# Modulation in plain fp32, attention maxima on the whole array, values weighed in groups of up to three

## The reference, cut to what matters

```python
mod = jax.nn.silu(c) @ w_mod[l] + b_mod[l]          # 1024 -> 3072, for c and for c_ctx
shift, scale, gate = jnp.split(mod, 3, axis=-1)
h = rms_norm(x, g_pre) * (1.0 + scale) + shift
z = h @ w_in                                        # q, k, v of both attentions, GLA, gates
s = jnp.einsum('bkgqd,bksd->bkgqs', q, k) * scale   # per head; sample queries see the cache too
p = jax.nn.softmax(s, axis=-1)
o = jnp.einsum('bkgqs,bksd->bkgqd', p, v)
o_c = rms_norm(o_c, c_out_gain)                     # the linear attention's output
x_new = x + gate * rms_norm(mixed @ w_out, g_post)
```

## Time and profile before

| what | us |
|---|---|
| time, median of 3 runs | 2437.39 (2436.99 to 2437.45) |
| the profiled execution | 2432.47, its span 2430.8 |
| modulation, layer 1 and 2 | 9.9 to 65.9, 1225.5 to 1275.9 |
| projection, layer 1 | 72 to 441 |
| attention, layer 1 | 536 to 1073 |
| PE busy in the span | 2159.8 (89%) |
| DVE, ACT, POOL busy | 1395.5, 961.3, 902.0 |

### The profile page before, as it was taken

How to read it: one execution, slowest core, us unless ns; L and a number is a source line. 1 busy time by engine, 2 the same in 40 slices (tenths; PEclk the granted TensorE clock), 3 DMA queues, 4 the chain that set the end, 5 groups by cost and what they waited for, 6 DMA issues and landing times. The chain is left out here.

```text
span 2430.8 us, 29142 instructions
## 1 busy us (share of the span) xinstructions
PE 2159.8 (89%) x10645; PEld 1453.8 (60%) x10645; DVE 1395.5 (57%) x2271; ACT 961.3 (40%) x1910; POOL 902.0 (37%) x490
## 2 busy tenths in 40 slices
PE   4799999888999999959958999998889999999598
PEld 3578888654444444427736789886544444444286
DVE  5668200585666666686556672006856666666864
ACT  5432221424555555541254322214255555555321
POOL 0211111324666666650002111113256666666600
PEclk8999999888999999979978999998899999999799
DMA  7232221110001000023373322211100010000333
GB/s 262 100 118 87 65 69 58 37 42 7 18 19 31 18 16 15 13 92 105 107 256 110 112 87 61 72 59 33 42 7 18 19 31 19 19 19 7 104 104 104
DMA packets 196825, 155.79 MB, mean 64 GB/s; under 512 B 125053, under 2 KB 150081, under 8 KB 196673
## 3 DMA queue, kind: packets, MB, share of 16 engines
q1 hardware_dynamic: 196672, 153.82, 21.2%
HBM read 115.37 MB, written 38.42 MB: 63 GB/s over the span
## 5 line engine op out<-in xcount | busy, mean ns | idle before, releaser
L1176 POOL TENSOR_TENSOR prob_sums<-prob_sums,probs 128x1024 f32<-128x1024 f32 x224 | 537.4, 2399 | 113.0 <-ACT probs L1365 93.2
L1365 ACT ACTIVATE probs<-scores 128x512 f32<-128x512 f32 x672 | 363.5, 605 | 388.1 <-PE scores L1246 205.8
L1426 DVE TENSOR_REDUCE neg_max_parts<-work 128x1 f32<-128x512 f32 (+1 forms) x640 | 398.3, 683 | 203.3 <-PE work L1225 202.4
L526 POOL TENSOR_TENSOR w_lo<-w_stage,w_hi 128x512 fp32r<-128x512 f32 (+1 forms) x112 | 134.5, 1234 | 828.5 <-ACT w_hi L461 828.5
L428 PE MATMUL z_acc<-w_hi,h_hi 128*128 128x512 f32 (+1 forms) x640 | 237.5, 371 | 12.0 <-DVE h_lo L545 8.1
L428 PE MATMUL z_acc<-w_hi,h_lo 128*128 128x512 f32 (+1 forms) x640 | 234.6, 367 | 0.0
L428 PE MATMUL z_acc<-w_lo,h_hi 128*128 128x512 f32 (+1 forms) x640 | 234.4, 366 | 0.0
L850 DVE MEMSET k_stackB<- 128x24 f32 (+1 forms) x4 | 0.9, 218 | 346.6 <-PEq L312 346.6
L1173 POOL TENSOR_TENSOR prob_sums<-probs 128x1024 f32<-128x1024 f32 x32 | 76.3, 2384 | 320.3 <-ACT probs L1365 320.3
L1463 DVE RECIPROCAL recip_sums<-work 128x512 f32<-128x512 f32 x32 | 107.5, 3358 | 144.4 <-PE work L1282 144.4
L428 PE MATMUL z_acc<-h_hi,w_lo 128*128 128x512 f32 (+1 forms) x528 | 187.0, 354 | 0.0
(11 more groups left out here) (244 smaller groups left out, 3894.8 us busy)
## 6 DMA issues: line engine op xcount, KB each, us to landing
mod_w<-in_w_mod SPq DMA_DIRECT2D x24, 1024.0 KB, 7.2
w_stage<-in_w_in SPq DMA_DIRECT2D x96, 256.0 KB, 3.0
z_scratch<-z_out SPq DMA_DIRECT2D x60, 256.0 KB, 2.0
cv<-u_scratch SPq DMA_DIRECT2D x20, 512.0 KB, 6.4
u_scratch<-z_out SPq DMA_DIRECT2D x32, 256.0 KB, 2.0
out_y_sample<-y_tiles SPq DMA_DIRECT2D x16, 512.0 KB, 5.2
q_rawA<-z_scratch SPq DMA_DIRECT2D x16, 320.0 KB, 4.1
vB<-z_scratch SPq DMA_DIRECT2D x16, 320.0 KB, 3.3
```

What stands on the lines that cost most here:

```text
L526: pool.tensor_tensor(w_lo[:, n % RING, 0:cols], stage[:, n % STAGES, 0:cols], w_hi[:, n % RING, 0:cols].bitcast(F32), ALU.subtract).then_i ...
L1176: ins = pool.tensor_tensor(a, a, pr[:, n % NPB, :], ALU.add)
L1365: act.activation(pr[:, n % NPB, c * NB:(c + 1) * NB], sc[m % SCORE_BANKS][:, :], ACT.Exp, scale=SCALE[u]).then_inc(s["a_exp"], 1)
L1426: dve.tensor_reduce(dst, src, AX_X, ALU.max, negate=True).then_inc(s["a_wkdve"], 1)
```

## The change

In the modulation `w_mod` stays whole in SBUF and is multiplied as plain fp32: 48 matmuls of 32 output columns, four of them at four column positions of the array. No rounding, no subtraction. SP issues all big loads at once, the shift and scale columns first, the gate columns last; ACT issues the 18 small ones. In the attention, `scan` goes: each piece 6 to 26 is one matmul over the whole array (128 rows for A, 96 for B). DVE copies pieces 3 to 5 instead of ACT. The maximum is one row instead of two. The steps are weighed in groups of 2, 3, 3, 2 and 1, the pieces are placed by `SLOTS`, `probs` has eight tiles, and `prompt_output` follows the maxima. To make room, three small tiles share the space of `recip_sums`, and `gla_norm` takes one token tile at a time. The prologue makes a small matrix `sel` for the turns, and the halves of `q_stackA2` and `kTA2` change places. Cut to its core:

```diff
@@ modulation_block @@
+            def load_w(k, c0, c1):
+                sp.dma_start(w[:, k, c0:c1], io["w_mod"][bass.ds(l, 1), k * P:(k + 1) * P, c0:c1].rearrange("a p n -> (a p) n")
+                             ).then_inc(s[f"m_w{k}" if c0 == 0 else f"m_g{k}"], 16)
+
+            load_w(0, 0, HEAD)
+            f.load_x(sp, 0)
+            for k in range(1, KD):
+                load_w(k, 0, HEAD)
+            f.load_x(sp, 1)
+            for k in range(KD):
+                load_w(k, HEAD, 3 * D_MODEL)
+            f.load_w(sp, 0, STAGES)
...
+            def products(pair, first, end):
+                for k in (2 * pair, 2 * pair + 1):
+                    pe.wait_ge(s[f"m_w{k}" if first == 0 else f"m_g{k}"], 16)
+                for a in range(first, end):
+                    for c in range(2):
+                        for r in range(2):
+                            x = 32 * (2 * c + r)
+                            n0 = (2 * a + c) * NB
+                            mm = pe.matmul(acc[a][x:x + 32, :], cond[:, 2 * pair + r, :], w[:, 2 * pair + r, n0:n0 + NB],
+                                           start=(pair == 0), stop=(pair == KD // 2 - 1), tile_position=(0, x))
+                    if pair == KD // 2 - 1:
+                        mm.then_inc(s["m_used"], 1)
...
+            pe.wait_ge(s["m_cond"], 2)
+            products(0, 0, 2)
+            pe.wait_ge(s["m_small"], 16 * 18)
+            pe.transpose(bias_tr, rows[:, :], per["ident"][0:NT + 2 * KD, 0:NT + 2 * KD]).then_inc(s["m_tr"], 1)
+            products(1, 0, 2)
+            f.turn(pe, 0)
+            products(2, 0, 2)
+            products(3, 0, 2)
+            turn(0)
+            turn(1)
+            for pair in range(KD // 2):
+                products(pair, 2, 3)
+            turn(2)
...
+            for dst, src in loads:
+                act.dma_start(dst, src).then_inc(s["m_small"], 16)
+            f.square(act, 0)
+            act.wait_ge(s["m_dot"], 2)
+            act.activation(dots[:, :], dots[:, :], ACT.Exp).then_inc(s["m_exp"], 1)
+            for a in range(PARTS):
+                act.wait_ge(s["m_used"], a + 1)
+                act.copy(parts[:, a, :], acc[a][:, :]).then_inc(s["m_evac"], 1)
+                if a == 1:
+                    f.square(act, 1)
...
+            def add_bias(out, a):
+                for g in range(2):
+                    do(dve.tensor_tensor(out[:, g, :].rearrange("p (c m) -> p c m", c=2), cols[a][:, :, :, g].rearrange("p m c -> p c m"),
+                                         bcols[:, a * KD:(a + 1) * KD].rearrange("p (c m) -> p c m", c=2), ALU.add))
...
@@ attention @@
-GROUPS = ((0, 1), (2, 3), (4, 5), (6, 7), (8, 9))
+GROUPS = ((0, 1), (2, 3, 4), (5, 6, 7), (8, 9))
 LAST = 10
 UNITS = 2 * A_HEADS
 PREP = 30
 PREP_Q, PREP_MAX, PREP_LAST = 3, 6, 27
-NPB = 6
+NPB = 8
 DIRECT = 1
 SCORE_BANKS, WORK_BANKS = 3, 4
 CHUNKS = 2 * KT_S + 1
-PROMPT_USE = 18
+PROMPT_USE = 27
+SLOTS = (((0, 2), (2, 2), (4, 2), (6, 2)), ((8, 2), (10, 2), (12, 2), (14, 3)), ((17, 3), (20, 3), (23, 4)))
...
-        nm = sb("neg_max", [P, T])
         rs = sb("recip_sums", [P, NB])
-        rsp = sb("recip_prompt", [P, P])
-        csq = sb("c_squares", [P, 2, C_HEADS * C_DV])
-        stats = sb("c_stats", [P, 3, T, C_HEADS])
+        rsp, csq = rs[:, 0:P], rs[:, 0:C_HEADS * C_DV]
+        stats = rs[:, 3 * P:3 * P + 3 * T * C_HEADS].rearrange("p (a t h) -> p a t h", a=3, t=T)
...
-        m_cols = {A: qst2[:, :, 0:2], B: qst[B][:, :, 3 * B_QK:KR[B]]}
+        m_cols = {A: qst2[:, :, HEAD_DIM], B: qst[B][:, :, 3 * B_QK]}
...
+                if i == PREP_MAX:
+                    wait_read(pe, prep_use(p, PREP_MAX - 1))
+                    if fresh(u, h):
+                        wait_read(pe, prep_use(p, PREP_Q - 1))
...
+                    m, rows = i - PREP_MAX, P if u == A else 3 * B_QK
+                    if m < 2 * TS:
+                        parts = [(m // 2, (m % 2) * NB, NB)]
+                    else:
+                        q0 = 2 * (m - 2 * TS)
+                        keys0 = 2 * NB if q0 < TS else KT_S * P
+                        parts = [(q0, keys0, SEQ), (q0 + 1, keys0, SEQ)]
+                    for x, (t, k0, n) in enumerate(parts):
+                        mm = pe.matmul(bank[:, x * SEQ:x * SEQ + n], qT[u][0:rows, tile_rows(t)], kT[u][0:rows, k0:k0 + n],
+                                       start=True, stop=True)
                 mm.then_inc(s["a_work"], 1)
-
-            def max_parts(m):
-
-                if m < 2 * TS:
-                    return [(m // 2, (m % 2) * NB, NB)]
-                q0 = 2 * (m - 2 * TS)
-                keys0 = 2 * NB if q0 < TS else KT_S * P
-                return [(q0, keys0, SEQ), (q0 + 1, keys0, SEQ)]
-
...
-                banks = [work_bank(pe, prep_use(p, i)) for i in pair]
-                parts = [max_parts(i - PREP_MAX) for i in pair]
-                for x in range(len(parts[0])):
-                    for r, bank in enumerate(banks):
-                        t, k0, n = parts[r][x]
-                        rows = slice(r * w, (r + 1) * w)
-                        keys = kT2 if u == A and r else kT[u]
-                        mm = pe.matmul(bank[:, x * SEQ:x * SEQ + n], qT[u][rows, tile_rows(t)], keys[rows, k0:k0 + n],
-                                       start=True, stop=True)
-                        if x == len(parts[0]) - 1:
-                            mm.then_inc(s["a_work"], 1)
...
                 for g in range(len(GROUPS) - 1):
-                    pieces(nxt, 6 * g, 2)
-                    ahead(p, GROUPS[g + 1][0])
-                    pieces(nxt, 6 * g + 2, 2)
-                    ahead(p, GROUPS[g + 1][1])
-                    pieces(nxt, 6 * g + 4, 2)
+                    for piece, step in zip(SLOTS[g], GROUPS[g + 1]):
+                        pieces(nxt, *piece)
+                        ahead(p, step)
+                    pieces(nxt, *SLOTS[g][-1])
                     for i in GROUPS[g]:
                         weigh(p, i)
-                pieces(nxt, 24, 2)
                 ahead(p, LAST)
-                pieces(nxt, 26, 1)
                 for i in GROUPS[-1]:
                     weigh(p, i)
                 pieces(nxt, PREP_LAST, PREP - PREP_LAST)
...
-                        if i in (1, 2, 3):
-                            for x in range(2 * i - 2, 2 * i):
+                        if i in (1, 2):
+                            for x in range(2 * i - 2, min(2 * i, PREP_Q)):
...
+                for i in range(PREP_Q, PREP_MAX):
+                    cols = slice((i - PREP_Q) * NB, min((i - PREP_Q + 1) * NB, TOK))
+                    dve.wait_ge(s["a_work"], worked(p, i))
+                    dve.tensor_copy(qT[u][:, cols], wk[prep_use(p, i) % WORK_BANKS][:, 0:cols.stop - cols.start]
+                                    ).then_inc(s["a_wkdve"], 1)
                 for i in range(PREP_MAX, PREP_LAST):
-                    if p and i == PROMPT_USE:
-                        prompt_output(p - 1)
...
-                dve.tensor_reduce(nm[:, 0:TS], nmx[:, 0:TS, :], AX_X, ALU.min).then_inc(s["a_own"], 1)
-                dve.wait_ge(s["a_own"], 2 * p + 1)
-                mc = m_cols[u]
-                dve.tensor_copy(mc[:, :, 0], nm[:, :]).then_inc(s["a_own"], 1)
-                dve.wait_ge(s["a_own"], 2 * p + 2)
-                dve.tensor_tensor(mc[:, :, 1], nm[:, :], mc[:, :, 0].bitcast(F32), ALU.subtract).then_inc(s["a_nm"], 1)
+                dve.tensor_reduce(m_cols[u][:, 0:TS], nmx[:, 0:TS, :], AX_X, ALU.min).then_inc(s["a_nm"], 1)
+                if p:
+                    prompt_output(p - 1)
...
+                wait_read(dve, prompt_use(p))
...
+                dve.wait_ge(s["a_out"], UNITS)
                 oc = mid["oc"]
-                for t in range(0, T, 2):
-                    do(dve.tensor_tensor(csq[:, :, :], oc[:, t:t + 2, :], oc[:, t:t + 2, :], ALU.mult))
-                    ins = dve.tensor_reduce(stats[:, 0, t:t + 2, :], csq[:, :, :].rearrange("p t (h e) -> p t h e", h=C_HEADS), AX_X,
-                                            ALU.add)
-                    if t + 2 < T:
+                for t in range(T):
+                    do(dve.tensor_tensor(csq, oc[:, t, :], oc[:, t, :], ALU.mult))
+                    ins = dve.tensor_reduce(stats[:, 0, t, :], csq.rearrange("p (h e) -> p h e", h=C_HEADS), AX_X, ALU.add)
+                    if t + 1 < T:
```

More of the change, by code:

```diff
@@ L264, in _ @@
-            f.square(act, 1)
+            C = C_HEADS * C_DK
+            gw = per["gate_w"]
+            loads = [(rows[0:NT, :], layer(io["b_mod"]).rearrange("a (m p) -> (a m) p", p=P)),
+                     (rows[NT:NT + KD, :], layer(io["g_pre"]).rearrange("a (m p) -> (a m) p", p=P)),
+                     (rows[NT + KD:, :], layer(io["g_post"]).rearrange("a (m p) -> (a m) p", p=P))]
+            loads += [(lams[:, i, :], layer(io[name]).broadcast_to([P, B_QK]))
```

(46 more changed lines are left out.)

188 lines of the change are left out of this document (57 added, 131 removed).

## The result

The change made the kernel slower: a median of 2447.97 us (2447.09 to 2449.76, 5 runs) against 2437.12 (2434.42 to 2437.45, 5 runs) in the same session, a ratio of 1.0048 (95% interval 1.0033 to 1.0062). The profiled execution's span is 2446.7 us at a mean granted clock of 0.942, against 2430.8 at 0.950.

The account below looks back on a forecast made before the run. PE was taken to bound the attention, with DVE's loop close behind, and queued loads the modulation; -22.5 - 25.6 + 15.4 + 7 = -25.7 gave 2406.8 profiled, 2412 us as median, forecast range 2395 to 2428, overall range 2364 to 2436.

Parts of the forecast that it names:

- B units: Attention units followed by an A unit: 30.3 us against 29.22, +1.1 each, +15.4 for 14; bounds -1.5 to +3.
- the modulation: Both layers' modulation bound by the load stream: -14.1 and -8.4, together -22.5; bounds -30 to -9.
- A units: Attention units followed by a B unit: 31.55 us against 33.17, -1.6 each, -25.6 for 16; bounds -2.9 to 0.
- unit 15: Last unit of each layer: ten half-size squares and sums in `gla_norm`, +3.5 per layer, +7 together; bounds +2 to +10.
- the wait behind `split_hi`: B unit: `split_hi` holds ACT for 1.6 us and so PE for 1.3.
- the clock falls: Rival: PE's new waits in B units bring back 1.2 GHz, 14 x 2.8 = 39, 2451 us; chance 0.10.
- lies between: B unit: PE's wait, 1.9 us beside 1.3, lies between harmless sub-microsecond waits and the 7.82 followed by a slow score.
- pieces and scores to 21.75: A unit layout: after three steps weighed to 17.35, PE's pieces and scores end 21.75 us into the unit.
- Worth little in PE time: Whole-array maxima in place of side-by-side pairs: 21 x 0.23 = 4.8 us for about 6.0 of PE time.
- PE waits for them after its first products, with 20 us to spare: Modulation: PE's wait for the small loads issued by ACT was to leave 20 us to spare.
- a rival with that size: Modulation doesn't get its stream: column tiles run serially or small loads hold all up; -9, 2425 us; chance 0.12.
- POOL and the copies: DVE's three query copies take 1.65 us; rival: POOL slows each by 0.9, +81, 2493 us, chance 0.03.

Follow-up runs that it names:

- filled_wait: Kernel after with the last score ahead of the first maxima made seven times over, into the same place; 2444.9 us (ratio to before 1.0032).
- late_pieces: Kernel after with the first two pieces of maxima moved behind the weighing of tiles 0 and 1; 2405.22 us (ratio to before 0.9876).
- whole_only: Kernel before with the maxima as whole-array matmuls in the same places and the query turn copied whole by ACT; 2412.7 us (0.9901).
- mod_late: Kernel before with the new modulation alone, its small-load wait and bias turn moved behind the fourth pair of products; 2416.8 us (0.9924).
- norm_pairs: Kernel after with the squares of the c branch made two tiles at a time, as in before; 2447.26 us (ratio to before 1.0051).
- q_on_act: Kernel after with the first query turns copied by ACT again instead of DVE; 2438.86 us (ratio to before 1.0014).
- whole_best: whole_only with the modulation of mod_late and ACT's square root moved from step 5 to step 8 of the last unit; 2388.82 us (0.9813).

## Why the prediction was wrong, step by step

The prediction put the profiled execution 25.7 below before; it came out 15.9 above. The 41.6 between are made of these terms: ordinary B units 12 x (3.26 - 1.1) = 26, the modulation 11, A units with the starts of the attention 10, less 3 for the two fresh units and less 2 for unit 15 and the rest.

**B units: the mechanism was right, two sizes were off.** PE's wait for the copies, which was to end 6.6 us into the unit, ended at 6.70; the first weighing, at 7.26, came at 7.38; the wait behind `split_hi`, 1.3, was 1.15; DVE's pitch of 0.61 held. At full clock the unit still took 31.03, not 30.3: DVE paced the last pieces, and the weighing behind them began at 21.8 (672.44 in filled_wait), 0.7 later than laid out. The rest is the rival *the clock falls*, to which I had given 0.10: it came true in eleven of twelve B units. Its time, 2451, is close to the 2448 partly by chance: I priced the fall at 2.8 us in each of fourteen units, filled_wait shows 1.6, and the time missing there was lost in the modulation and the A units. The step that failed is "lies between": a wait of 1.9 us beside one of 1.3 was put at one in ten, although the trace of before spoke against it. In its fresh B unit PE waits 1.16 us for ACT, and the weighing shortly behind takes 3.33 in place of 1.94; layer 2 has the same (1.15 and 2.78), and in its unit 15 a wait of 1.33 did it:

```profile
788.03 0.50 PE L1248 MATMUL scores<-qT2B,kTB 128*128 128x512 f32 x1 [1.16 <-ACT probs L1365]
...
789.09 3.33 PE L1262 MATMUL att_out<-probs,vB 128*64 128x512 f32 x8
...
2249.93 3.27 PE L1262 MATMUL att_out<-probs,vB 128*64 128x512 f32 x8 [1.33 <-DVE oa L1442]
```

The prediction had read the waits of ordinary units, which are under a microsecond, and the 7.82 of unit 15.

The larger omission is that the layout itself showed PE idle from 4.7 to 6.6 with a weighing ready at 4.9, right behind it in PE's order. late_pieces took those 1.8 us away, and the 1.6 with them.

**A units: -0.8 in place of -1.6.** Against the forecast, "pieces and scores to 21.75", the prompt's products wait for DVE's reading of the last pieces until 22.7 (703.93 in unit 4):

```profile
703.93 0.66 PE L1231 MATMUL work<-probs,vA 128*64 128x128 f32 x8 [0.19 <-DVE neg_max_parts L1376]
```

The step that failed is that I followed DVE's pace in the B unit and not in the A unit. The length itself can be had: whole_only, with other slots and groups, has 31.66 against the forecast's 31.55. "Worth little in PE time" held: PE's busy time in that unit is 0.4 below that of before, and most of the gain is the wait of 0.92 for ACT's copies, which the prediction had in its layout.

**The modulation: -11.3 in place of -22.5.** The stream ran as forecast, near 400 GB/s. The failed step is "PE waits for them after its first products, with 20 us to spare": the loads land 18 us after their last issue, beside SP's stream, and the work behind the wait is 16 us. A bound of -9 for the small loads and a rival with that size were in the text; but I gave them as a matter of the stream, which the loads might hold up, and it was PE's order. mod_late restores -18.2. Of the remaining 4, 2.4 stand at the end of layer 1 (54.16 against the forecast's 51.8), most of it the tail at the lower clock, and 1.1 in layer 2 (42.9 us after the first load against 41.8).

**Unit 15: right.** +3.5 forecast, +3.8 and +2.7 measured. Three squares of 2.0 stand among the ten, and DVE's sums end at 19.8 us into the unit, where five ended at 17.1. norm_pairs gave back 3.0 and 1.6 of it.

**POOL and the copies: right.** The three took 1.62 us beside POOL's additions; 1.65 was forecast.

## What to carry over

When an engine moves to a place where it will wait, look first at what stands behind the wait in its own order and is already ready: here one weighing issued ahead of two pieces turned a loss of 11 us into a gain of 31. Lay out every loop in every kind of unit, the engine that follows included, and charge a group of work with the idle time that it makes for the engine fed from its buffers. Where PE is the bound, an idle stretch is paid twice, as the wait and as the lower clock behind it, and the second part can cost as much as the first.

## What the hardware showed beyond that

- 1.72 to 1.84 us without a matmul brought PE's granted clock from its upper level (2.4 GHz) to its lower (1.2 GHz) in eleven of the twelve ordinary B units of after; 1.83 us in the twelfth did not, nor did 0.83 and 0.46 in the ordinary units of q_on_act and filled_wait. In unit 15 a wait of 1.3 us ahead of the first weighing was harmless in layer 1 of before, and not in layer 2 of before or in layer 1 of whole_best. In the fresh units 1.16 and 1.15 brought the clock down in before, and so did 0.65 and 0.53 close together in filled_wait, which did nothing in after. So the length of the wait alone doesn't decide. PE in unit 15 of before:

```profile
1040.39 1.94 PE L1262 MATMUL att_out<-probs,vB 128*64 128x512 f32 x8 [1.33 <-DVE oa L1442]
```

And of whole_best:

```profile
1022.01 3.62 PE L1232 MATMUL att_out<-probs,vB 128*64 128x512 f32 x8 [1.32 <-DVE oa L1408]
```

- Useless matmuls paid where they filled a wait: six of them made an ordinary B unit 1.6 us shorter. Where they filled none, in the fresh units, these grew by 2.9.
- Eighteen small loads issued from ACT's queue while SP's queue held 1 MB loads landed 18 us after the last of them was issued, when most of the stream was through. No run here issued them without that stream, so what held them isn't shown.
- A matmul with 96 rows of contraction took as long as one with 128 (0.46 for two of 512 columns).
